# Seven of the sixteen tiles of layer 0's gate modulation go from TensorE to VectorE

## The reference

```python
def modulate(x, norm_g, ada):
    shift, scale, gate = jnp.split(ada, 3, axis=-1)
    return rmsnorm(x, norm_g) * (1 + scale) + shift, gate

def mixer_layer(...):
    h, gate = modulate(x, norm_g, (c_act @ w_ada + b_ada)[:, None, :])
    hc, gate_c = modulate(xc, norm_g, cc_act @ w_ada + b_ada)
    u = h @ w_in
    uc = hc @ (w_in[:, :OFF_MEM_END] if last else w_in)
    ...   # conv branch, RG-LRU branch, windowed attention, each times its own SiLU gate
    x = x + gate * (jnp.concatenate([y_conv, y_lru, y_attn], axis=-1) @ w_out)
    ...   # the same for xc in layer 0
```

## Time and profile before

| | |
|---|---|
| median of 3 runs | 1241.06 us |
| the profiled execution's own time | 1241.5 us |
| its span in the trace | 1239.7 us |
| mean granted TensorE clock | 0.995 |
| PE busy | 1198.3 us, 97% |
| DVE busy | 852.1 us, 69% |
| ACT busy | 555.6 us, 45% |
| chain of waits | PE 88%, SP's queue 4%, DMA 4%, DVE 2%, ACT 2% |

### The profile page before, as it was taken

One profiled execution on the slowest core, in us unless ns is written; L12 is line 12 of the kernel. 1 busy time (PEld: TensorE's weight loads), 2 busy tenths in 40 slices (PEclk: granted clock), 3 DMA queues, 4 the chain that ended last, 5 costly groups with the idle time before them and its releaser, 6 DMA issues.

```text
span 1239.7 us, 16341 instructions
## 1 busy us (share of the span) xinstructions
PE 1198.3 (97%) x6518; PEld 958.5 (77%) x6518; DVE 852.1 (69%) x1291; ACT 555.6 (45%) x873; POOL 10.2 (1%) x13
## 2 busy tenths in 40 slices
PE   2899999999999999999999999999999999999996
PEld 1556777767778788886888887988978988899885
DVE  5444546767656677663768998695899977657664
ACT  5222446662224434454442222454865455575542
POOL 0000100000000000000000001000000000000000
PEclk9999999999999999999999999999999999999998
DMA  9999856556753442221538887444432634325552
GB/s 335 350 348 348 257 200 250 204 204 241 277 215 133 144 162 84 69 68 68 197 122 350 324 329 261 128 140 135 138 106 77 222 136 149 122 100 202 189 171 68
DMA packets 80892, 236.32 MB, mean 191 GB/s; under 512 B 9392, under 2 KB 54192, under 8 KB 59440
## 3 DMA queue, kind: packets, MB, share of 16 engines
q1 hardware_dynamic: 80816, 235.27, 53.9%
HBM read 230.54 MB, written 2.10 MB: 188 GB/s over the span
## 4 chain that ended last, share of the span: by engine, by line
PE 88%; SPq 4%; DMA 4%; DVE 2%; ACT 2%; issue 0%; DVEq 0%; ACTq 0%
PE psum_block L837 20%; PE psum_block L838 20%; PE psum_block L839 20%; PE psum_block L834 5%; SPq L609 3%; PE psum_ada L663 3%; PE psum_block L835 2%; DMA raw<-in_w_ada 2%; PE psum_scores L919 1%; PE psum_scores L906 1%; PE psum_scores L939 1%; PE psum_scores L869 1%; PE psum_ada L710 1%; DMA bd<-in_w_ada 1%; DMA glu<-in_w_ada 1%; PE psum_misc L966 1%
## 5 line engine op out<-in xcount | busy, mean ns | idle before, releaser
L837 PE MATMUL psum_block<-h_parts,w_hi 128*128 128x512 f32 (+1 forms) x1408 | 494.3, 351 | 0.3 <-DVE h_parts L1413 0.3
L838 PE MATMUL psum_block<-h_parts,w_hi 128*128 128x512 f32 (+1 forms) x1408 | 485.3, 345 | 0.0
L839 PE MATMUL psum_block<-h_parts,w_lo 128*128 128x512 f32 (+1 forms) x1408 | 485.3, 345 | 0.0
L1421 DVE TENSOR_TENSOR w_lo<-raw,w_hi 128x1024 fp32r<-128x1024 f32 x210 | 254.6, 1223 | 257.8 <-ACT w_hi L1061 257.7
L1061 ACT ACTIVATE w_hi<-raw 128x1024 fp32r<-128x1024 f32 x210 | 220.1, 1056 | 413.5 <-PE psum_block L839 354.4
L837 PEld LDWEIGHTS psum_block<-h_parts,w_hi 128*128 128x128 f32 x1408 | 266.6, 189 | 51.5 <-issue 16.8
L838 PEld LDWEIGHTS psum_block<-h_parts,w_hi 128*128 128x128 f32 x1408 | 266.8, 189 | 33.5 <-issue 2.6
L839 PEld LDWEIGHTS psum_block<-h_parts,w_lo 128*128 128x128 f32 x1408 | 266.7, 189 | 32.4
L1706 DVE SCALAR_TENSOR_TENSOR Y<-glu,small,Y 128x512 f32<-128x512 f32 (+1 forms) x240 | 130.4, 612 | 0.0
L834 PE MATMUL psum_block<-h_parts,w_hi 128*128 128x512 f32 x240 | 84.8, 399 | 0.0
L835 PE MATMUL psum_block<-h_parts,w_lo 128*128 128x256 f32 x240 | 67.4, 281 | 0.0
(11 more groups left out here) (228 smaller groups left out, 1349.1 us busy)
## 6 DMA issues: line engine op xcount, KB each, us to landing
raw<-in_w_blocks SPq DMA_DIRECT2D x105, 1024.0 KB, 4.9
raw<-in_w_ada SPq DMA_DIRECT2D x71, 1024.0 KB, 7.0
glu<-in_w_ada SPq DMA_DIRECT2D x10, 1024.0 KB, 9.9
bd<-in_w_ada SPq DMA_DIRECT2D x10, 1024.0 KB, 9.5
qreg<-in_w_blocks SPq DMA_DIRECT2D x8, 896.0 KB, 11.6
kv<-in_w_ada SPq DMA_DIRECT2D x5, 1024.0 KB, 11.9
Y<-in_xT SPq DMA_DIRECT2D x8, 512.0 KB, 7.8
T<-in_xT SPq DMA_DIRECT2D x16, 256.0 KB, 7.0
```

The lines of the kernel that those rows point to most:

```text
L837: mm(ps[:, cols], hi, hh[:, k, t], start=(at == 0), stop=False)
L838: mm(ps[:, cols], hi, hl[:, k, t], start=False, stop=False)
L839: last = mm(ps[:, cols], lo, hh[:, k, t], start=False, stop=(at == DT - 1))
L1421: V.tensor_tensor(wl[:, u % 4, 0:n], raw_of(item)[:, cols], wh[:, u % 4, 0:n].bitcast(F32), ALU.subtract).then_inc(*C.up("lo", u))
```

## The change

Tiles 9 to 15 of layer 0's gate are no longer multiplied on PE. DVE multiplies each by the two columns of `cstat` and adds it to two accumulators of 128 x 2048: the latents' in `Y[:, 8:16, 0:LAT]` (one instruction of 2048 elements a partition), the context's half in `Y[:, 2:4, :]` and half in `bd` (two instructions of 1024). They are done in block 7 (tiles 9, 10), 8 (11, 12), 10 (13) and 14 (14, 15): tile 9 right after the first `lo` of block 7, the others at the end of the block's DVE work. PE keeps tiles 0 to 8, in blocks 9, 11, 12, 13 (two each) and 15 (one). After the last one, `gate0_sum` sums the accumulators over partitions into the same bank with eight matmuls. Layer 1's shift tiles follow in blocks 16 to 23, a block later than before; its four scale tiles on PE stay in 24 and 26. ACT's first attention gate and `split_kv` now also wait for the sum.

```diff
+GATE0_ON_DVE = {7: [9, 10], 8: [11, 12], 10: [13], 14: [14, 15]}
+GATE0_ON_PE = {9: [0, 1], 11: [2, 3], 12: [4, 5], 13: [6, 7], 15: [8]}
+GATE0_SUM = 15
...
@@ ada_plan
-    rest = ([(0, GATE, k) for k in range(DT)] + [(1, SHIFT, k) for k in range(DT)]
-            + [(1, SCL, k) for k in range(DT - on_dve)])
-    single = GATE1_AT - DT
-    plan = {b: [rest.pop(0) for _ in range(2)] for b in range(OPEN[0], GATE1_AT)
-            if rest and (b < single or (b - single) % 2)}
+    rest = [(1, SHIFT, k) for k in range(DT)] + [(1, SCL, k) for k in range(DT - on_dve)]
+    plan = {b: [(0, GATE, k) for k in tiles] for b, tiles in GATE0_ON_PE.items()}
+    plan[GATE0_SUM] += [(0, GATE, DT - 1)]
+    first = GATE0_SUM + 1 + DT // 2
+    for b in range(GATE0_SUM + 1, GATE1_AT):
+        if rest and (b < first or (b - first) % 2 == 0):
+            plan[b] = [rest.pop(0) for _ in range(2)]
...
@@ stream
-                s += [("ada", *a) for a in plan.get(b, []) if b != SCALE_SUM] + [("gate", k) for k in gates.get(b, [])]
+                s += [("ada", *a) for a in plan.get(b, []) if a[2] != DT - 1 or a[:2] not in SUMMED]
+                s += [("gate0", k) for k in GATE0_ON_DVE.get(b, [])] + [("gate", k) for k in gates.get(b, [])]
...
@@ used
+            if item[0] == "gate0":
+                return C.at("gate0_acc", item[1], 2)
...
@@ tensor
+            def gate0_sum():
+
+                pe.wait_ge(*C.at("pick_set"))
+                pe.wait_ge(*C.at("gate0_acc", DT - 1, 2))
+                for i in range(2):
+                    for j in range(4):
+                        part = (Y[:, 8 + 2 * j:10 + 2 * j, 0:LAT] if i == 0 else Y[:, 2 + j, :] if j < 2
+                                else bd[:, 1, 4 * (j - 2):4 * (j - 1), :])
+                        last = mm(psA[32 * j:32 * j + 32, :], pick[:, 32 - i:64 - i], part,
+                                  start=False, stop=(i == 1), tile_position=(0, 32 * j))
+                last.then_inc(*C.up("ada_mm", 0, GATE, DT - 1))
...
@@ scalar
                 elif kind == "ag":
+                    if l == 0 and i == 0:
+                        act.wait_ge(*C.at("ada_mm", 0, GATE, DT - 1))
...
             def split_kv(l):
+                act.wait_ge(*C.at("ada_mm", 0, GATE, DT - 1))
...
@@ vector
+            def gate0_acc(k):
+
+                w = raw_of(("gate0", k))
+                dve.wait_ge(*arrived(("gate0", k)))
+                parts_of = ((0, Y[:, 8:16, 0:LAT], w.rearrange("p (m t) -> p m t", t=LAT)),
+                            (1, Y[:, 2:4, :], w[:, 0:2 * TOK].rearrange("p (m t) -> p m t", t=TOK)),
+                            (1, bd[:, 1, :, :], w[:, 2 * TOK:4 * TOK].rearrange("p (n c) -> p n c", c=P)))
+                first = k == min(min(tiles) for tiles in GATE0_ON_DVE.values())
...
+                for n, (i, acc, x) in enumerate(parts_of):
+                    c = cstat[:, c_at(k) + i:c_at(k) + i + 1]
+                    if first:
+                        V.tensor_scalar(acc, x, c, None, ALU.mult).then_inc(*C.up("gate0_acc", k, n))
+                    else:
+                        dve.wait_ge(*C.ago("gate0_acc", 2))
+                        stt(acc, x, c, acc, ALU.mult, ALU.add).then_inc(*C.up("gate0_acc", k, n))
...
                 if gb + 2 < GLOB and not in_halves(gb):
                     lo(unit(0, gb + 2, 0))
+                if gb == OPEN[0]:
+                    gate0_acc(GATE0_ON_DVE[b][0])
...
                 if l == 0:
+                    for k in GATE0_ON_DVE.get(b, [])[1 if b == OPEN[0] else 0:]:
+                        gate0_acc(k)
                     for k in SCALE_ON_DVE.get(b, []):
                         scale_acc(k)
```

More of the change, by code:

```diff
@@ L136, in ada_plan @@
     return plan
+SUMMED = [(0, GATE), (1, SCL)]
 def gate1_plan():
@@ L599, in _ @@
                     src = io["w_ada"][1, item[1] * P:(item[1] + 1) * P, GATE * D:(GATE + 1) * D]
+                elif item[0] == "gate0":
+                    src = io["w_ada"][0, item[1] * P:(item[1] + 1) * P, GATE * D:(GATE + 1) * D]
                 elif item[0] == "scale":
@@ L1042, in _ @@
                     misc.append(("pw_out", l, CT - 1))
[L1043 to L1046, removed]
+                for a in PLAN.get(b, []) if l == 0 else []:
+                    if a == (0, GATE, DT - 1):
+                        gate0_sum()
+                    elif a == (1, SCL, DT - 1):
+                        scale_sum()
+                    else:
                         ada_mm(*a)
@@ L1455, in gate_acc @@
                     stt(acc, w, cstat[:, c_at(k):c_at(k) + 1], acc, ALU.mult, ALU.add).then_inc(*C.up("gate_acc", k))
+            def gate0_acc(k):
[6 more added lines that the diff above has]
+                if first:
+                    dve.wait_ge(*C.at("h_lo", 0, DT - 1, 1))
+                    dve.wait_ge(*used(last_of(BD_SLOT)))
+                for n, (i, acc, x) in enumerate(parts_of):
+                    c = cstat[:, c_at(k) + i:c_at(k) + i + 1]
+                    if first:
+                        V.tensor_scalar(acc, x, c, None, ALU.mult).then_inc(*C.up("gate0_acc", k, n))
+                    else:
+                        dve.wait_ge(*C.ago("gate0_acc", 2))
+                        stt(acc, x, c, acc, ALU.mult, ALU.add).then_inc(*C.up("gate0_acc", k, n))
             def scale_acc(k):
```

## The result

The changed kernel takes 1255.32 us (median of 4 executions, 1254.49 to 1256.36), the kernel before 1241.24 us (4 executions, 1240.91 to 1241.56). The ratio is 1.011 with a 95% interval of 1.0098 to 1.0123: slower by 14.1 us, where 11.9 were forecast. The profiled execution is the fastest of the four: 1254.49 us, span 1252.7, which is 13.0 over the span before. In the last experiment one execution of six took 3090 us, far from the other five (1236.42 to 1238.00), and its median is taken over all six.

The account below looks back on a forecast made before the run. PE, busy 97% of the span, was taken as the bound. Saving - 4.6, waits + 7.2, + 3.9 and + 2.0, slow clock + 3.4 gave + 11.9 us: 1253.0 us on the median, range 1247 to 1257.

Parts of the forecast that it names:

- How many loads wait: The opening said three of PE's loads wait for slots that DVE holds.
- PE's saving, 4.6 us: On PE, seven tiles less at 0.93 us (6.5 us) and one sum more (1.85 us): net 4.6 us less work.
- A tile costs DVE 4.56 us: On DVE, one multiply-add of 2048 elements (2.26 us) and two of 1024 (1.15 each); bounds 2.6 and 4.7 us.
- The waits at blocks 9, 11 and 15: PE waits at these blocks' ends for tile loads into slots DVE holds: 7.2, 3.9 and 2.0 us.
- What stays: The 1.1 us `ada_out` wait moves to block 16's end; new waits for the sum and later shift steps cost 0.
- The scan in block 10: Expected over early, so DVE's `lo` starts 1.15 us after block 10's end, where it was 1.54 before.
- The clock, 3.4 us: PE's clock falls behind the first and second waits, 1.7 us lost each; bounds 0 and 5.1 us.
- That the clock holds: Rival: PE's waits come but its clock does not fall; + 8.5 us, 1249.6; chance 0.2.
- That the loads land in time: Rival: PE's tile loads come without waits and the saving stays; faster by 4.6 us, 1236.4; chance 0.07.
- that the tiles are cheap: Rival: a DVE tile takes 2.6 us, so waits shrink, no clock fall; + 0.5 us, 1241.5; chance 0.06.
- That DVE becomes the bound: Rival: tiles push DVE's `lo` so far that PE waits for weights too; adds 2 to 6 us, about 1257; chance 0.07.
- the prediction's doubt about its third wait: At block 15's end, whether a 2.0 us gap between dense matmuls also makes PE's clock fall; not counted in the forecast.

Follow-up runs that it names:

- the last experiment: Seven on DVE and nine on PE, respread over the blocks, with DVE's tiles neither loaded nor accumulated: 1237.41 us, ratio 0.9964 to the kernel before.
- the last two experiments: Changed kernel's tiles respread, DVE with none in block 13, one in 14: 1237.29 us; the same with DVE's tiles neither loaded nor accumulated: 1237.41 us.
- the shorter tile: Changed kernel with the context's half left out, so DVE does only the one instruction of 2048 elements a tile: 1241.74 us, ratio 1.0004 to the kernel before.
- the other order: Changed kernel with DVE's tiles 11 and 12 in block 8 moved before the LRU's taps: 1249.78 us, ratio 1.0065 to the kernel before.
- the first table: Changed kernel with the same seven DVE and nine PE tiles spread, nearly one each a block: 1245.47 us, ratio 1.0031 to the kernel before.
- the kernel with filled gaps: Changed kernel with extra matmuls on a free bank before PE's four waiting tiles (18, 18, 20, 10): 1252.73 us, ratio 1.0089 to the kernel before.

## Why the prediction was right

Point by point, in its own steps:

- *How many loads wait.* The opening speaks of three of PE's loads behind DVE's slots; the sum goes on with four (tiles 0, 1, 3 and 8), and four there were.
- *PE's saving, 4.6 us.* Nearly: the last two experiments gave 4.2 and 4.1 us. Both traces have a wait of 0.6 us for ACT near the end (1223 us) that the trace before doesn't have.
- *A tile costs DVE 4.56 us.* Nearly: 4.65 (170.17 to 174.82). The instruction of 1024 elements, which the trace before didn't have, takes 1.28 us and not the 1.22 of a `lo` of that size, as the groups of DVE show:

```profile
L1504 DVE SCALAR_TENSOR_TENSOR Y<-raw,cstat,Y 128x2048 f32<-128x2048 f32 x6 | 14.1, 2343 | 0.0
L1504 DVE SCALAR_TENSOR_TENSOR Y<-raw,cstat,Y 128x1024 f32<-128x1024 f32 x6 | 7.7, 1277 | 0.0
```

- *The waits at blocks 9, 11 and 15.* Right in place, number and size, 13.1 us forecast and 13.5 measured. The cause is shown by the shorter tile and by the other order, not only by the trace.
- *What stays.* Right: the wait for `ada_out` is 1.1 us again, one block later, and the shift's later blocks cost nothing.
- *The scan in block 10* was not over early, as I had it: PE's late block 10 held `hi`, and DVE idled 8.1 us before the block's first `lo`, at 205.95. It changed nothing: the second `lo` started at 211.39, when both the scan and its `hi` (210.30 + 1.06) were done, 1.26 us after the end of block 10, where 1.15 was forecast.
- *The clock, 3.4 us.* The term that was mis-sized. Two falls came, as forecast, but they cost 4.4 us. I had priced a fall by the one stretch before, 1.7 us, and the first cost just that; in the second one PE was at work for some 6 of its 7 us, and it cost 2.75.
- *The rest.* The forecast was 2.3 us short of the median (1253.0 against 1255.32): 1.0 is the clock's, 0.4 the waits'. The rest is spread that no trace explains: the changed kernel's four executions lie within 1.9 us, at mean clocks of 0.987 to 0.990; those of the kernel before lay within 0.7 us here and within 1.5 beside the experiments.
- *Rivals.* That the clock holds is ruled out (0.51 and 0.57 in the stretches). That the loads land in time, and that the tiles are cheap, are ruled out by the four waits and the 4.65. That DVE becomes the bound is ruled out for the changed kernel by PE's waits, none of which is for weights, and by the other order; in the first table DVE was late for the sum.

## What to carry to other kernels

In a ring of buffers that several engines consume, ask for each load whose slot it takes over and when that engine will be done: work that is free in the sum of an idle engine can still hold a slot that the bottleneck needs. Give the slot of the slow consumer to the next item of the same consumer, or to one that has a block of lead, and follow this through the whole table, since two items in one step shift the turn. An order or a table is a cheap thing to try again: here the same work took 1255.3, 1249.8, 1245.5 and 1237.3 us.

## What the runs showed of the hardware

- Around gaps of some 2 us the clock went either way. It fell to 0.5 in or right behind PE's gaps of 2.14 and 2.34 us in the first table and of 2.68 us in the other order. It stayed at 1.00 behind gaps of 2.10 us in the changed kernel, 1.96 in the other order, and 1.06 to 1.63 in the kernel with the cheaper tile. So the prediction's doubt about its third wait was in place. The fall that it had read at 36 us in the kernel before came behind a gap of 2.13 us too:

```profile
36.64 1.76 PE L710 MATMUL psum_ada<-bd,cstat 128*32 128x512 f32 x8 [2.13 <-DMA bd<-in_w_ada]
```

- The size of a gap alone doesn't tell: at block 9 of the changed kernel the clock held through the gap of 3.83 us and the 0.93 us of tile 0, and fell some 0.5 us into the next gap. The Trainium skill, "TensorE: Matmul & The Clock Gate", Part 1, has only activity release the slow clock; the trace agrees in that the clock fell while PE stood idle here, and stayed at 1.00 where 3.3 and 3.4 us of filling matmuls stood in the same two gaps.
- A fall is not of one length: some 3 us for the first one in the reordered kernel and for both in the first table, some 7 us for both of the changed kernel's.
- The first stage, which is the same in all of these kernels, ends at different times in their single profiled executions: block 7's transpose starts at 162.46 to 164.30 us. Two traces are therefore compared from that point on, and a difference of 1 us between spans need not come from the edit.
- A load of 1 MB that PE waited for landed 4.7 to 5.0 us after its issue in the changed kernel, the other order and the kernel with the cheaper tile, and once, in the kernel with filled gaps, after 6.3.
